# Both feed-forward layers: the norm's factor applied when PSUM is drained, first rows rounded in the phase ahead, scratch of the tables in two PSUM banks

## The reference

```python
def rmsnorm(x, g):
    y = x * lax.rsqrt(jnp.mean(x * x, axis=-1, keepdims=True) + EPS) * g
def swiglu(h, w_in, w_out):
    gu = h @ w_in
    return (jax.nn.silu(gu[..., :FFN_HIDDEN]) * gu[..., FFN_HIDDEN:]) @ w_out
x = x + mixer(rmsnorm(x, norm_mix_g[i]))
x = x + swiglu(rmsnorm(x, norm_ffn_g[i]), w_ffn_in[i], w_ffn_out[i])
```

## Time and profile before

| | us |
|---|---|
| median of 3 runs | 3339.38 |
| lowest and highest | 3334.08, 3341.84 |
| profiled execution, its own time | 3344.76 |
| its span, first to last instruction | 3343.0 |
| PE busy | 3157.8 (94%) |
| DVE busy | 1959.9 (59%) |
| ACT busy | 813.2 (24%) |
| POOL busy | 853.0 (26%) |

### The profile page before, as it was taken

One profiled execution on the slowest core, in us unless ns is written; L12 is line 12 of the kernel. 1 busy time (PEld: TensorE's weight loads), 2 busy tenths in 40 slices (PEclk: granted clock), 3 DMA queues, 4 the chain that ended last, 5 costly groups with the idle time before them and its releaser, 6 DMA issues.

```text
span 3343.0 us, 69153 instructions
## 1 busy us (share of the span) xinstructions
PE 3157.8 (94%) x29901; PEld 2972.2 (89%) x29901; DVE 1959.9 (59%) x4351; ACT 813.2 (24%) x1842; POOL 853.0 (26%) x762
## 2 busy tenths in 40 slices
PE   5999999999999999889999999978898999999998
PEld 4879898988888888789999999966897999999997
DVE  5556666666666666678777777369223443444345
ACT  3334343444434343320100111123102100000001
POOL 2202121212112121123333323333232333333331
PEclk7979999999999999999999999988899999999999
DMA  3111212121111121101222222257221111111111
GB/s 99 47 59 48 71 55 73 53 67 62 64 60 60 60 66 53 47 26 53 66 86 73 72 86 73 72 203 238 61 49 32 45 51 45 45 51 45 45 51 64
DMA packets 110431, 223.46 MB, mean 67 GB/s; under 512 B 23984, under 2 KB 58288, under 8 KB 109104
## 3 DMA queue, kind: packets, MB, share of 16 engines
q1 hardware_dynamic: 81504, 177.65, 17.0%
q10 hardware_dynamic: 28624, 41.38, 3.9%
HBM read 177.86 MB, written 41.14 MB: 66 GB/s over the span
## 4 chain that ended last, share of the span: by engine, by line
PE 87%; DVE 9%; ACT 1%; issue 1%; POOL 1%; DMA 1%; SPq 0%; POOLq 0%; DVEq 0%; ACTq 0%
PE ps L224 34%; PE ps L695 16%; PE ps L1464 15%; PE ps L781 5%; PE ps L729 2%; PE ps L756 1%; PE ps L722 1%; PE ps L707 1%; PE ps L749 1%; PE ps L762 1%; PE ps L769 1%; PE ps L713 1%; PE ps L1425 1%; PE ps L240 1%; DVE x L1248 1%
## 5 line engine op out<-in xcount | busy, mean ns | idle before, releaser
L224 PE MATMUL ps<-hhi,whi 128*128 128x344 f32 x2376 | 763.3, 321 | 6.0 <-DVE hlo L348 3.5
L224 PE MATMUL ps<-hhi,wlo 128*128 128x344 f32 x2376 | 760.4, 320 | 0.0
L224 PE MATMUL ps<-hlo,whi 128*128 128x344 f32 x2376 | 759.6, 320 | 0.0
L2345 POOL TENSOR_TENSOR wtick<-wtick 128x1 f32<-128x1 f32 x213 | 51.4, 241 | 2346.6 <-PE ps L224 791.4
L2348 POOL TENSOR_TENSOR wlo<-wraw,whi 128x1024 fp32r<-128x1024 f32 x213 | 532.5, 2500 | 17.1
L224 PEld LDWEIGHTS ps<-hhi,whi 128*128 128x128 f32 x2376 | 448.2, 189 | 9.1 <-DVE hlo L348 3.7
L224 PEld LDWEIGHTS ps<-hhi,wlo 128*128 128x128 f32 x2376 | 447.9, 188 | 0.0
L224 PEld LDWEIGHTS ps<-hlo,whi 128*128 128x128 f32 x2376 | 447.4, 188 | 0.1
L695 PE MATMUL ps<-hhi,whi 128*128 128x344 f32 x1152 | 385.6, 335 | 1.8 <-DVE tg L1121 1.8
L695 PE MATMUL ps<-hhi,wlo 128*128 128x344 f32 x1152 | 369.5, 321 | 0.0
L695 PE MATMUL ps<-hlo,whi 128*128 128x344 f32 x1152 | 369.0, 320 | 0.0
(11 more groups left out here) (425 smaller groups left out, 4954.0 us busy)
## 6 DMA issues: line engine op xcount, KB each, us to landing
wraw<-in_w SPq DMA_DIRECT2D x213, 512.0 KB, 3.5
dwork<-keep_rows SPq DMA_DIRECT2D x64, 256.0 KB, 3.7
S<-in_sin ACTq DMA_DIRECT2D x16, 512.0 KB, 3.9
drw<-keep_del SPq DMA_DIRECT2D x32, 256.0 KB, 3.4
out_sout<-S ACTq DMA_DIRECT2D x16, 512.0 KB, 2.7
keep_u<-hraw SPq DMA_DIRECT2D x8, 580.0 KB, 4.4
uu<-keep_u SPq DMA_DIRECT2D x8, 580.0 KB, 5.8
keep_tab<-cp ACTq DMA_DIRECT2D x8, 576.0 KB, 5.4
```

Source lines behind the costliest of these rows:

```text
L224: ins = nc.tensor.matmul(out, w, r[:, kt, blk(n)], start=k == 0, stop=k == 3 * KT - 1)
L2345: G.tensor_tensor(wtick[:, 1:2], wtick[:, 0:1], wtick[:, 0:1], ALU.add)
```

## The change

- **Form.** ffn0 takes the form that ffn1 has: both layers call `raw_act`, `raw_dve`, `raw_block`, `raw_sums`, `raw_total`, and drain g and u with `rated`. `project_pair` and the normed blocks are no longer used there.
- **Rounding ahead.** Blocks n = 0 and 1 of `hhi` and `hlo` are made in the phase before: at the end of mix (DVE: one `lower` behind each `add_x` of n = 1 and 2) and at the end of glu (last m, `high` on ACT and `lower` on DVE between the blocks). Only n = 2 is left in the feed-forward phase.
- **No meeting.** After mix and glu PE, ACT and DVE no longer meet. ACT and DVE meet with the old phase (`meet_old`) before their squares; PE waits for each bank's old drain instead (`drains`).
- **Order on PE:** g0, u0, g1, the sums, u1, total 0, g2, total 1, u2, total 2, where before it was four blocks, the sums, g2, two totals, u2, one total in ffn1.
- **Banks.** In ffn0 the turn has 6 banks; banks 4 and 5 (`SCRATCH`) serve the sums and totals and then DVE's scratch of the tables. `cp` is computed through two halves, which makes 10 instructions of what were 6.
- **f = 10.** The share at the start of an f is given only for f = 1 to 9.

```diff
@@ raw_act(a, ph, gi)
             nc.scalar.preload_act_table_set(LOGEXP)
-            high(0)
-            high(1)
+            a.meet_old()
             for n in range(NC3):
                 for kt in range(0, KT, 2):
                     raw_square(a, n, kt)
-            high(2)
+            for kt in range(KT):
+                high(a, gi, 2, kt)
@@ end of mix_act
+            a.ahead("ffn0")
+            for n in range(2):
+                for kt in range(KT):
+                    a.after_old("DVE", f"{e}.x{kt}.{n}")
+                    high(a, 1, n, kt)
+            a.back()
@@ end of mix_dve
             for n in (1, 2):
                 for m in range(KT):
                     add_x(e, m, n)
+                    v.ahead("ffn0")
+                    lower(v, 1, n - 1, m)
+                    v.back()
@@ rotation
-        def rotation(p):
+        def rotation(p, order=tuple(range(8)), drains=None):
...
-                b = turn % 8
+                b = order[turn % len(order)]
+                if b in drains:
+                    p.after_old(*drains.pop(b))
@@ ffn_pe
+                if ph == "ffn0":
+                    turning = [b for b in left if b not in SCRATCH]
+                    take = rotation(p, turning, {b: left_drains[b] for b in turning})
...
+                raw_block(0, 0)
+                raw_block(1, 0)
+                raw_block(0, 1)
+                raw_sums(p, norm_bank)
+                raw_block(1, 1)
+                raw_total(p, 0, norm_bank)
+                raw_block(0, 2)
+                raw_total(p, 1, norm_bank)
+                raw_block(1, 2)
+                raw_total(p, 2, norm_bank)
...
-   project(p, unit(ph, f, 2 * j), lambda n: take(*(("DVE", f"tg{f}.{j}.{n}") if late else ("ACT", f"sg{f}.{j}.{n}"))), f"g{f}.{j}.")
+   project(p, unit(ph, f, 2 * j), lambda n: take("DVE", f"tg{f}.{j}.{n}"), f"g{f}.{j}.")
@@ ffn_dve
-                        if f and not late:
+                        if 0 < f < SR + 2:
                             aside(11000 if f == 1 else 9300)
-                        for j in range(2) if late else ():
+                        for j in range(2):
                             for n in range(NC3):
                                 rated(sg, "tg", "g", f, j, n)
@@ table_dve
-                    a0, a1 = tmp[:, 0, :, 0:n], tmp[:, 1, :, 0:n]
+                    a0, er1, ei1 = a_[:, :, 0:n], ee[:, 0, :, n:2 * n], ee[:, 1, :, n:2 * n]
                     yield v.spend((4 * n + 160), V.tensor_tensor(a0, er, br, ALU.mult))
-                    yield v.spend((4 * n + 160), V.tensor_tensor(a1, ei, bi, ALU.mult))
-                    yield v.spend((4 * n + 160), V.tensor_tensor(ee[:, 0, :, n:2 * n], a0, a1, ALU.subtract))
+                    yield v.spend((4 * n + 160), V.tensor_tensor(er1, ei, bi, ALU.mult))
+                    yield v.spend((4 * n + 160), V.tensor_tensor(er1, a0, er1, ALU.subtract))
...
-                yield v.spend(736, V.tensor_tensor(t1[:, :, :, :], c4[0], l4[0], ALU.mult))
+                for w, s_ in zip(t1, halves):
+                    yield v.spend(400, V.tensor_tensor(w, c4[0][:, s_], l4[0][:, s_], ALU.mult))
@@ glu_act, m == 7 and n < 2, after sig7.n
+                        a.ahead("ffn1")
+                        for kt in range(KT):
+                            a.after_old("DVE", f"x{kt}.{n}")
+                            high(a, 3, n, kt)
+                        a.back()
@@ glu_dve, m == 7, after ab7.n
+                        add_gated(m, n)
+                        if n < 2:
+                            v.ahead("ffn1")
+                            for kt in range(KT):
+                                lower(v, 3, n, kt)
+                            v.back()
@@ program
-                    E.meet()
+                    if who == "POOL" or ph not in ("mix", "glu"):
+                        E.meet()
```

More of the change, by code:

```diff
@@ L168, in meet, with meet_old @@
                     value = plan.get((who, self.pfx + "end"), 0)
+                    if value:
+                        self.until(who, value)
+            def meet_old(self):
+                for who in sems:
+                    value = plan.get((who, self.old + "end"), 0)
                     if value:
@@ L402, in raw_dve @@
         def raw_dve(v, gi):
[L403 to L410, removed]
+            v.meet_old()
             for n in range(NC3):
@@ L924, in mix_pe @@
                     out_piece(e, m, n, take)
+            left[:] = [DENSE[(dense + k) % 7] for k in range(7)]
+            left_drains.update(held)
         def mix_act(a):
@@ L1410, in body @@
             def body(p):
[L1411 to L1436, removed]
-                else:
-                    sums(p, 0, take)
-                    sums(p, 1, take)
@@ L1441, in block_ready, with norm_bank @@
[L1441 to L1444, removed]
+                first = [unit(ph, 0, u) for u in range(2)]
+                if ph == "ffn0":
+                    turning = [b for b in left if b not in SCRATCH]
+                    take = rotation(p, turning, {b: left_drains[b] for b in turning})
+                    def norm_bank(who, name):
+                        if name == "ln2":
+                            p.after("ACT", "ln0")
+                        plan[("bank", p.pfx + name)] = SCRATCH[name in ("ln0", "ln2")]
+                        return SCRATCH[name in ("ln0", "ln2")]
+                else:
+                    take = norm_bank = rotation(p, (6, 7, 0, 1, 2, 3, 4, 5), {6: ("ACT", "sig6.1"), 7: ("ACT", "sig6.2"), **{n: ("DVE", f"ab7.{n}") for n in range(3)}, **{3 + n: ("ACT", f"sig7.{n}") for n in range(3)}})
@@ new lines, in body, with raw_block @@
+                at = [wait_weights(p, u) for u in first]
+                def raw_block(j, n):
+                    s = at[j]
+                    out = ps[:, take("DVE", f"{('tg', 'ub')[j]}0.0.{n}"), 0:NB]
+                    for kt in range(KT):
+                        p.after("DVE", f"lo{n}.{kt}")
+                        w_h = whi[:, s, kt * P:(kt + 1) * P]
+                        w_l = wlo[:, s, kt * P:(kt + 1) * P]
+                        for q, (w, r) in enumerate(((w_h, hhi), (w_h, hlo), (w_l, hhi))):
+                            ins = nc.tensor.matmul(out, w, r[:, kt, blk(n)], start=kt == 0 and q == 0, stop=kt == KT - 1 and q == 2)
+                    p.go(ins, f"{('g', 'u')[j]}0.0.{n}")
+                    plan[("PE", f"unit{first[j]}")] = p.n
@@ L1491, in body @@
             def body(a):
[L1492 to L1496, removed]
+                raw_act(a, ph, 1 if ph == "ffn0" else 3)
                 for f in range(NF + 1):
@@ L1504, in body @@
                             for n in range(NC3):
[L1505 to L1512, removed]
+                                a.after("DVE", f"tg{f}.{j}.{n}")
+                                a.go(nc.scalar.activation(sg[:, j, blk(n)], sg[:, j, blk(n)], AF.Silu), f"sg{f}.{j}.{n}")
                             if ph == "ffn0" and j == 0 and 0 <= f - 3 < SR:
@@ L1550, in body @@
                 V = nc.vector
[L1551 to L1555, removed]
+                raw_dve(v, 1 if ph == "ffn0" else 3)
                 def rated(dst, name, product, f, j, n):
@@ L2227, in glu_dve, with add_gated @@
             V = nc.vector
+            def add_gated(m, n):
+                v.after("DVE", f"ab{m}.{n}")
+                v.go(V.tensor_tensor(x[:, m, blk(n)], x[:, m, blk(n)], rf["ab"][:, 0, blk(n)], ALU.add), f"x{m}.{n}")
             k = 6
```

74 lines of the change are left out of this document (44 added, 30 removed).

## The result

The changed kernel takes 3375.5 us (median of 4 runs, 3371.3 to 3385.1) where the kernel before, run on the same chip, takes 3336.7 (4 runs, 3329.6 to 3341.8). The ratio is 1.0122, with a 95% interval of 1.009 to 1.0154: slower, by more than a measurement of this kernel is uncertain. The profiled execution of after took 3371.54 us (span 3369.6); that of before, 3344.76.

A forecast was written before the change was run, and what follows sets the result against it. PE was taken to bound ffn0's rounds, leaving the chain only at the two seams. Terms -14.9 - 7.3 + 24.5 + 16.9 + 1.7 + 11.2 = +32.1 on 3339.4 gave 3371.5 us, range 3335 to 3390.

The forecast's parts named there:

- Seam 1: Mix into ffn0, from the last mix piece to the third unit's start: 57.2 us before, to shrink by 14.9 us.
- Seam 2: Glu into ffn1, up to the third unit's start: 50.1 us before, to shrink by 7.3 us.
- Seven waits: ffn0 rounds 3 to 9: PE waits 3.5 us each for a DVE drain queued behind table instructions, +24.5 us.
- Rounds 0 and 1: First rounds of ffn0: PE waits 9.4 and 7.5 us for DVE's late drains, +16.9, plus 1.7 for slow clock.
- Clock behind the seven waits: ffn0 rounds 3 to 9: PE runs slow after each wait, 1.6 us lost each time, +11.2 us, between 0 and this.
- Sum: Whole kernel: all terms add to +32.1 us, giving 3371.5 us, 1.0% slower.
- case 4: The prediction's own case, with 0 to 11 us for the clock and 3.0 to 4.0 per wait: 3353 to 3379, chance 0.70.
- PSUM scratch: Table instructions in ffn0, four of each six now touching PSUM: no difference in time from SBUF assumed.
- POOL's hold: ffn0: POOL spares the new drains but can hold the product, 2.3 us a round, within 3 us of cover.
- rival 2: Waits bind in f = 0 and 1 only, as POOL's hold on PSUM-touching table instructions vanishes: -3.6 us, 3336, chance 0.08.
- The pessimistic rival: PSUM scratch is dear or DVE falls behind at the output pieces too: 3384 or 3391 us, chance 0.10.

The follow-up runs named there:

- e2: Changed kernel with the start share of table work in rounds 2 to 9 halved, 4300 of 9300 ns moved behind the three tg drains: 3341.9 us, ratio to before 1.0008.
- e1: Changed kernel with only DVE's order altered: table shares cut in thirds, one ahead of each tg drain: 3359.5 us, ratio to before 1.0064.
- e4: Changed kernel with the tables' scratch in one PSUM bank instead of two, the freed bank added so seven turn: 3343.0 us, ratio to before 1.0017.

## Why the prediction was right

It said slower by 1.0%, 3371.5 us; the ratio says 1.2%, and the place, the size and the count of the waits are those of the text. As a difference to before it had +32.1 us; the stages give +34.7, the medians +38.8 and the two profiled executions +26.8, so the closeness of the whole times is in part luck, and the terms are what bears it out. By its own steps:

- **Seam 1**: -14.9 predicted, -13.2 found. PE's start 3.95 us after mix was 4.23; the clock behind it took 2.5 us of 72 matmuls where I had 2.2; the totals 0.77 each, not 0.6.
- **Seam 2**: -7.3 and -6.8.
- **Seven waits**: 3.5 each and 3.4 found, 24.0 of 24.5. The sum behind it held in each part: the table share ran 16.3 us (16.45), the drain behind it, PE ready at 14.04 us into the round. Rounds 2 and 10 have none, as said.
- **Rounds 0 and 1**: 9.4 and 7.5 of waiting and 1.7 of clock predicted, 18.6. Found: 8.9, then 2.5 of slow clock in the 144 matmuls between the two waits (25.2 us instead of 22.7, below), then 5.0. The second wait was DVE's time minus PE's, and the slow clock had used up part of it: 2.5 + 5.0 = 7.5. Behind it 6.2 - 2.5 = 3.7 us went to the clock, where I had 1.7. The sum was right within 2 us; what I missed is its nature. I costed one more place in the queue, and it is a stretch in which DVE had no time left before the change and which PE now reaches 12.8 us nearer to it: most of seam 1's gain comes back as these waits.
```profile
1478.70:1503.90 25.20, 25.19 (x144) 24.95 (x144) 22.37 (x88) 2.71 (x6) 3.63 (x3) 0.90 0.07 22
```
- **Clock behind the seven waits**: 7 x 1.6 = 11.2 predicted. ffn0 grew by 54.7 us, 37.9 of them idle and 16.8 clock; without the seven waits (e2) it is 762.0 - 741.9 - 13.9 = 6.2. So the seven cost 10.6.
- **Sum**: -22.2 + 41.4 + 12.9 = +32.1 predicted; -20.0 + 37.9 + 16.8 = +34.7 by the stages. The bounds of case 4, 3353 to 3379, are wider than its terms: waits of 3.0 and no clock give 3355, waits of 4.0 with all of it 3375, since the seams and rounds 0 and 1 were given no width. The 3375.5 measured stands at that upper end.
- **PSUM scratch**: I took no difference. Mean ns of the tables' instructions by shape, in after:
```profile
L1791 DVE TENSOR_TENSOR ps<-ee,pwr 128x256 f32<-128x256 f32 x8 | 3.5, 432 | 0.3
L1792 DVE TENSOR_TENSOR ee<-ee,pwr 128x256 f32<-128x256 f32 x8 | 3.4, 425 | 0.3
L1790 DVE TENSOR_TENSOR ee<-ps,ee 128x256 f32<-128x256 f32 x8 | 3.4, 424 | 0.3
```
  The write to PSUM costs 7 ns of 425, the read nothing. The 5.3 us wait that an estimate from the Trainium skill ("VectorE: DVE Perf Modes", the TRN2 errata) gave did not come: 3.4. The estimate also counted too many: of the 28 instructions 14 read PSUM and 14 write it, and the Trainium skill's figure is for a PSUM source. With 14 the same estimate gives a wait of 4.4 us, which did not come either.
- **POOL's hold**: rival 2 let it vanish from the table instructions. It stayed: in f = 5 `ee<-ee,pwr` took 2.45 us at 1789.52 and a write to PSUM from two SBUF sources 2.07 at 1778.35, each beside a split of POOL (2.40 us from 1789.28 and 2.41 from 1777.97). And it moved onto the product, as said, once in this round:
```profile
1808.60 2.71 DVE L1608 TENSOR_TENSOR ab<-ab,sg 128x344 f32<-128x344 f32 x1
...
1821.95 1.36 DVE L1580 TENSOR_TENSOR sg<-ps,n_r 128x344 f32<-128x344 f32 x3
```
  It was free there: PE shows no wait behind it. The first tg(1) drain starts at 1821.95, 45.3 us into the round (from 1776.61), where I counted 48.2 for its end, and the pieces begin at 1829.80, 53.2 us into it, where I had 51.4: the cover ahead of them was some 7 us, not 3. e1 spent it and paid 2 us a round.
- **The pessimistic rival** (DVE behind at the pieces too) did not happen in after and did in e1 and, at half a microsecond a round, in e4. The mechanism was right and needed another order, or a PE that does not wait earlier in the round, to show.

## What to carry to other kernels

When an edit moves a bank's drain to an engine that carries background work in whole shares, find the share in the queue and count from its start to the drain, against the time at which the bank is needed: here that sum gave 3.5 us, and 3.4 came. A small mend in the order (half the share behind the drain) or one more buffer is then worth as much as the whole wait and its clock. And look at the other engines stretch by stretch before you start one of them earlier: DVE was at 59% over the whole span and full in two rounds (90% busy, no pause over 0.3 us). PE was brought forward by 13.2 us into these rounds and DVE's own work was not, and 8 to 14 us came back as waits in each of the orders that I tried.

## What the runs showed of the hardware

- After a PE pause of 3.4 us the granted clock was 0.57 over 4 us and 1.00 behind that, 1.6 us of 34.15 lost in three units; behind 4.2 and 4.4 us at the seams 2.5 and 1.6 us were lost. Taking the seven pauses away gave back 10.6 us beyond their length.
- A DVE instruction that writes PSUM takes as long as one that writes SBUF (432 and 425 ns on 128x256). Writing PSUM does not keep it free of POOL when both its sources are in SBUF: beside a split it took 2.07 us on 128x4, where the same line takes 0.18 us on 128x8 and on 128x16.
- Ten profiled executions reach the end of mix between 1394.8 and 1409.3 us, while PE's busy time up to 1390 is the same within 1 us in before, after, e1 and e4 (1288.3 to 1289.3). The order of the kernels in that column follows none of the edits. What it depends on stays open.
